# An expert stage's first block: empty products ahead of a gather's wait, a weight load ahead of it

## What is computed

```python
    le_g = jnp.take_along_axis(le, gsel[:, :, None], axis=1)[:, 0]
    ev, ei = lax.top_k(le_g, TOP_K)
    wts = jnp.take_along_axis(pg, gsel, axis=1) * jax.nn.softmax(ev, axis=-1)
    ...
    for e in range(N_EXPERTS):
        he = jax.nn.silu(h2 @ w_gate[e]) * (h2 @ w_up[e])
        out = out + combine[:, e:e + 1] * (he @ w_down[e])
```

## Time and profile before

| | us |
|---|---|
| median of 3 runs | 975.17 (972.69 to 975.19) |
| the profiled execution | 972.41 |
| its span in the profile | 970.6 |
| PE busy | 949.0 (98%) |
| VectorE busy | 700.3 (72%) |
| ScalarE busy | 493.1 (51%) |
| GpSimd busy | 190.1 (20%) |

### The profile page before, as it was taken

How to read it: one execution, slowest core, us unless ns; L and a number is a source line. 1 busy time by engine, 2 the same in 40 slices (tenths; PEclk the granted TensorE clock), 3 DMA queues, 4 the chain that set the end, 5 groups by cost and what they waited for, 6 DMA issues and landing times.

```text
span 970.6 us, 14838 instructions
## 1 busy us (share of the span) xinstructions
PE 949.0 (98%) x5402; PEld 818.1 (84%) x5402; DVE 700.3 (72%) x1063; ACT 493.1 (51%) x895; POOL 190.1 (20%) x153
## 2 busy tenths in 40 slices
PE   6999999999999999999999999999999999999996
PEld 5899999999999999999888886567777777777762
DVE  7467777789454544636666667779999999999986
ACT  7588777433322222322422314256666666666794
POOL 2000000000000000000030001325464646464414
PEclk9999999999999999999999999999999999999999
DMA  7214775524765554546833236899999999999994
GB/s 233 52 33 135 169 170 134 170 88 125 233 169 151 159 144 117 146 140 187 275 104 130 74 105 258 301 409 414 413 416 415 414 410 412 401 414 413 388 396 166
DMA packets 123477, 230.09 MB, mean 237 GB/s; under 512 B 71525, under 2 KB 84491, under 8 KB 114712
## 3 DMA queue, kind: packets, MB, share of 16 engines
q1 hardware_dynamic: 108078, 202.16, 60.2%
q0 software_dynamic: 15264, 26.92, 7.4%
q10 hardware_dynamic: 74, 0.20, 0.1%
HBM read 204.81 MB, written 53.11 MB: 266 GB/s over the span
## 4 chain that ended last, share of the span: by engine, by line
PE 92%; DMA 2%; DVE 2%; ACT 2%; issue 1%; POOL 1%; POOLq 0%; DVEq 0%; SPq 0%
PE psum L1184 34%; PE psum L2532 12%; PE psum L2181 9%; PE psum L2622 8%; PE psum L2536 5%; PE psum L2468 3%; PE psum L1207 2%; PE psum L2092 1%; PE psum L2516 1%; PE psum L2131 1%; PE psum L2589 1%; PE psum L1289 1%; PE psum L1276 1%; PE psum L1282 1%; PE psum L1293 1%
## 5 line engine op out<-in xcount | busy, mean ns | idle before, releaser
L1184 PE MATMUL psum<-hh,wh 128*128 128x350 f32 x672 | 222.9, 332 | 1.6 <-DVE hl L866 1.6
L1184 PE MATMUL psum<-hh,wl 128*128 128x350 f32 x672 | 217.6, 324 | 0.0
L1184 PE MATMUL psum<-hl,wh 128*128 128x350 f32 x672 | 216.9, 323 | 0.0
L1184 PEld LDWEIGHTS psum<-hh,wh 128*128 128x128 f32 x672 | 127.3, 189 | 3.0 <-issue 2.0
L1184 PEld LDWEIGHTS psum<-hl,wh 128*128 128x128 f32 x672 | 127.2, 189 | 0.9
L1184 PEld LDWEIGHTS psum<-hh,wl 128*128 128x128 f32 x672 | 127.0, 189 | 0.0
L2506 DVE TENSOR_TENSOR wgu_lo<-wgu,wgu_hi 128x1536 fp32r<-128x1536 f32 x60 | 105.4, 1758 | 18.1 <-ACT wgu_hi L2501 17.7
L2501 ACT ACTIVATE wgu_hi<-wgu 128x1536 fp32r<-128x1536 f32 x60 | 89.3, 1489 | 4.1 <-DMA new_ssm_sample<-s_in 4.1
L2532 PE MATMUL psum<-wgu_hi,xgt_hi 128*128 128x512 f32 x180 | 85.6, 475 | 0.0
L1742 POOL IOTA r_iw<- 128x8 f32 x1 | 0.1, 143 | 407.2 <-DMA mixer_rows<-th 407.2
L2532 PE MATMUL psum<-wgu_lo,xgt_hi 128*128 128x512 f32 x180 | 70.8, 393 | 0.0
(11 more groups left out here) (395 smaller groups left out, 1910.4 us busy)
## 6 DMA issues: line engine op xcount, KB each, us to landing
wgu<-w_gate SPq DMA_DIRECT2D x34, 1024.0 KB
wgu<-w_up SPq DMA_DIRECT2D x34, 1024.0 KB
wd<-w_down SPq DMA_DIRECT2D x34, 1024.0 KB, 15.2
wst<-w_in SPq DMA_DIRECT2D x28, 512.0 KB, 4.4
ck<-qkv_rows SPq DMA_DIRECT2D x9, 702.0 KB
qkv_rows<-acc SPq DMA_DIRECT2D x12, 520.0 KB, 5.9
xb<-x SPq DMA_DIRECT2D x8, 512.0 KB, 4.4
wo<-w_out SPq DMA_DIRECT2D x8, 512.0 KB, 6.7
```

The lines of the kernel that those rows point to most:

```text
L1184: ins = mm(ps[:, c, 0:ZC], w[:, kk, :], a[:, kk, c * ZC:(c + 1) * ZC], start=(kk == 0 and q == 0), stop=(kk == KD - 1 and q == 2))
```

## The change

On PE, block 0: all nine empty products run at the end of the router (before three there, four behind the turn), and `totals` runs ahead of the wait for the gather. The turn of block 0 signals after its first four transposes; ScalarE's first copy waits for that, its second for the whole turn. The signal uses the semaphore `ninth`, now named `passed`. `gate_up` gets an argument `halves`, with which it waits for one copy, then for the other at the middle; `mid` passes it for block 0. On SyncE, gate and up of the third expert are loaded before the wait for the gathers, behind the wait for the residual rows.

```diff
     def sync_more(sp):
+        sp.wait_ge(b.x1_out.sem, b.x1_out.at(16 * T))
+        load_gate_up(sp, b, io, expert_of(2), 2)
         for k in range(2):
             sp.wait_ge(b.gathered[k], 16)
         load_down(sp, b, io, expert_of(1), 1)
-        sp.wait_ge(b.x1_out.sem, b.x1_out.at(16 * T))
-        load_gate_up(sp, b, io, expert_of(2), 2)
         load_down(sp, b, io, expert_of(2), 2)
...
-        idle_products(pe, 3)
+        idle_products(pe, 9)
...
-    def turn(pe, q, k):
+    def turn(pe, q, k, half_turned=None):
...
+            if g == 0 and half_turned is not None:
+                ins.then_inc(half_turned, 1)
         ins.then_inc(q.turned.sem, 1)
...
-    def copy_turned(act, q, p, n):
-        act.wait_ge(q.turned.sem, q.turned.at(n + 1))
+    def copy_turned(act, q, p, n, half_turned=None):
+        if half_turned is None:
+            act.wait_ge(q.turned.sem, q.turned.at(n + 1))
+        else:
+            act.wait_ge(half_turned.sem, half_turned.at(4))
...
         for g in range(2):
+            if g == 1 and half_turned is not None:
+                act.wait_ge(q.turned.sem, q.turned.at(n + 1))
...
-    def gate_up(pe, q, p, n, k, part=range(KD)):
+    def gate_up(pe, q, p, n, k, part=range(KD), halves=False):
         if part[0] == 0:
-            pe.wait_ge(q.xt_ok.sem, q.xt_ok.at(2 * n + 2))
+            pe.wait_ge(q.xt_ok.sem, q.xt_ok.at(2 * n + (1 if halves else 2)))
         for kk in part:
+            if halves and kk == KD // 2:
+                pe.wait_ge(q.xt_ok.sem, q.xt_ok.at(2 * n + 2))
...
+                if isinstance(x.e, int) and x.e == 0:
+                    route.totals(pe)
                 pe.wait_ge(gathered[x.k], 16 * (x.r + 1))
-                turn(pe, x.q, x.k)
-                if isinstance(x.e, int) and x.e == 0:
-                    route.idle_products(pe, 4)
-                    route.totals(pe)
+                turn(pe, x.q, x.k, route.passed.sem if isinstance(x.e, int) and x.e == 0 else None)
...
             def mid(x):
...
-                    gate_up(pe, x.q, x.p, x.n, x.k)
+                    gate_up(pe, x.q, x.p, x.n, x.k, halves=isinstance(x.e, int) and x.e == 0)
```

More of the change, by code:

```diff
@@ L1643, in route_parts @@
                                                   s("rwf_ok"))
-    weighted, ninth, x1_1, sq_1 = (s.again("x1_weighted"), s.again("ninth_tile_parts"), s.again("x1_first_half"),
+    weighted, passed, x1_1, sq_1 = (s.again("x1_weighted"), s.again("tensor_passed"), s.again("x1_first_half"),
                                     s.again("x1_first_squares"))
@@ L1718, in sync @@
         residual_stored(sp, T - 2)
-        sp.wait_ge(ninth.sem, ninth.at(2))
+        sp.wait_ge(passed.sem, passed.at(2))
         load_gate_up(sp, b, io, expert_of(0), 0)
-        sp.wait_ge(ninth.sem, ninth.at(3))
+        sp.wait_ge(passed.sem, passed.at(3))
         load_down(sp, b, io, expert_of(0), 0)
@@ L2001, in vector @@
                 dve.wait_ge(x_in[0], 16 * (T // 2 + 1))
-                dve.wait_ge(ninth.sem, ninth.at(1))
+                dve.wait_ge(passed.sem, passed.at(1))
                 add_half(0).then_inc(x1_1.sem, 1)
@@ L2133, in last_products @@
                     if c == 1 and i in (3, 5):
-                        ins.then_inc(ninth.sem, 1)
-                ins.then_inc(ninth.sem if c == 0 else prod, 1)
+                        ins.then_inc(passed.sem, 1)
+                ins.then_inc(passed.sem if c == 0 else prod, 1)
         for t in range(T - 1):
@@ L2222, in route_parts @@
     f.vector_extra, f.vector_tables, f.tensor_extra = vector_extra, vector_tables, tensor_extra
-    f.idle_products, f.totals = idle_products, totals
+    f.totals, f.passed = totals, passed
     return f
@@ L2829, in front_ @@
                 else:
-                    copy_turned(act, x.q, x.p, x.n)
+                    copy_turned(act, x.q, x.p, x.n, route.passed if isinstance(x.e, int) and x.e == 0 else None)
             def half(x):
```

## The result

| | median us | runs | ratio to before (95% interval) |
|---|---|---|---|
| before | 975.22 | 20 | |
| after | 979.65 | 20 | 1.0049 (1.0026 to 1.0072) |

Single runs of most kernels here lie 10 us or more above the rest, and the ratios leave the farthest out, so a ratio can differ from that of the medians.

A forecast was written before the change was run, and what follows sets the result against it. The prediction took PE to bound the kernel (busy 98% of the span, 92% of the chain). Its terms, -1.87 (PE) + 2.5 (gather) + 1.3 (clock), summed to +1.9 us: 977.1 us, range 973.0 to 979.8.

The forecast's parts named there:

- the likeliest case: Whole kernel: 977.1 us, +1.9 on the median, between -0.5 and +2.9 us; chance 0.50.
- slower beyond 0.3%: Rival: first gather waits for all the new loads, landing 615.1; +3.9 us, or +5.6 with a second low stretch; chance 0.26.
- Steps (1) and (2), PE: First gather's landing to first gate and up product: empty products and totals move ahead, first copy starts earlier; -1.87 us.
- Step (3), room behind it: Later PE steps: VectorE's gated rows and third expert's low part come in time, so the 1.87 us gain passes on.
- the 0.1 us for block 0's gated rows: Second PE step of block 0: VectorE finishes `he` at 624.92, PE needs it at 625.02; it just fits.
- The room of 2.2 us at the third expert: Third expert's weights: VectorE's first low part ready by 638.5, PE takes it at 640.72.
- Step (4), the gather: Third expert's loads fill the DMA engines as the first gather is issued; it lands about 613.5, +2.5 us.
- the upper bound of +4.1: First gather: new loads end at 612.5, then the gather takes 2.6 us alone and lands at 615.1.
- the other half: Half of the 5.1 us full-queue cost, put on sharing the engines; little of it paid, since the load ends at 612.5.
- The rows of the running sum: Same sort of gather elsewhere in the trace: lands 2.6 us after issue at kernel's end, 7.7 to 8.6 in expert stage.
- Step (5), the clock: PE idle 3.1 us before the delayed landing, so a low clock stretch falls on the first products; +1.3 us.
- The load's lead: DMA engines gain about 2.5 us for the sample store and fourth expert; worth nothing, as PE doesn't wait for either.

The follow-up runs named there:

- e1_pe_part: The changed kernel with SyncE's order of before put back, so only the work on PE and ScalarE is moved; 974.11 us against 974.36, ratio 1.0007.
- e7: The kernel before, storing only 0.25 of the 2 MB of the sample state; 970.59 us against 973.75, ratio 0.9978.
- e3: As e1_pe_part, with the halves argument also passed in both product calls of `begin`; ratio to before 1.0013.
- e8: As e1_pe_part, storing only 0.25 of the 2 MB of the sample state; 971.15 us against 973.75 for before, ratio 0.9971.
- e2: The kernel before with only SyncE's order changed: third expert's gate and up ahead of the wait for the gathers; 976.95 us against 974.36, ratio 1.0038.
- e4: The changed kernel with only the third expert's gate (1 MB) ahead of the wait for the gathers; 977.33 us against 974.36, ratio 1.0004.
- e11: The kernel before with one more 2 MB DMA copy on SyncE near the end of the expert stage; 982.2 us against 974.01, ratio 1.0077.

## Why the prediction was wrong

The range of 973.0 to 979.8 held 979.65, but the likeliest case, a loss of 1.9 us that can't be told from no change, was wrong: the case "slower beyond 0.3%" with its 0.26 came true, and with the mechanism written there in the main: the gather was held up by the new loads beyond the point given. Only it didn't wait for the whole of them, its packets began while they still ran. Point by point:

- **Steps (1) and (2), PE**: forecast -1.87 us from landing to first product. e1_pe_part has 2.01 us there for the 1.83 forecast, so -1.69, right to 0.2 us; `begin` without `halves` cost 0.5 us as said. But 1.24 of it was the removal of a low stretch which not every execution has, as e7 shows; the forecast compared a start at the lower clock with one at the full clock and priced it as if each execution had it.
- **Step (3), room behind it**: the 0.1 us for block 0's gated rows was about right (e3 waits 0.35 with 0.5 more asked). "So a gain of 1.87 passes on" was the wrong sentence. I looked for the next late step up to block 2 and not at the end, where the DMA engines set the time: the earlier trace rows give DMA 2% of the chain, and I read that as PE alone. The room of 2.2 us at the third expert was right for a gain of 1.87 alone. In e1 the second low stretch was missing too, so PE came 3.5 us earlier and waited 1.25 for VectorE's low part. That part starts at R 31.8 in both kernels, since ScalarE waits there for the 2 MB sample store, which landed at R 30.3 in both:

```profile
640.77 0.47 PE L2541 MATMUL psum<-wgu_hi,xgt_hi 128*128 128x512 f32 x1 [1.25 <-DVE wgu_lo L2513]
```

- **Step (4), the gather**: the term that was mis-sized, and the main failure. +2.5 forecast, +4.9 measured (8.87 for 3.96), and above the upper bound of +4.1. The wait for data ahead came out as forecast, 2.6 measured up to the first packet for 2.55 (half of 5.1), by luck, since the halves were a guess. "Little of" the other half was wrong, with +2.3 measured. The bound let the load end at 612.5 and gave the gather 2.6 us alone from there; in fact it had the rest of the load and the later gathers beside it, and took 4.4 us from its first packet. The rows of the running sum, 7.7 to 8.6 us under a full queue, were the better estimate as they stood: 8.87, 8.38 and 7.85 in three kernels.
- **Step (5), the clock**: +1.3 forecast. In the profile of after the way from the turn of block 0 to that of block 1 took 8.85 us, against 5.48 in e8 at the full clock: +3.4. The stretch was three times 3.4 us, where the forecast had one and left a second open. Whether the longer idle time (5.5 us and not 3.1) or the missing products behind the turn made it so isn't shown: e2, idle for 6.5 us with these products in place, had two. By the ratios the share is about 2 us.
- **The sum** by what was measured from the router's table: -1.69 + 4.91 + 3.37 = +6.6, as the trace has it at block 1's turn, and +6.0 at the end. The medians give +4.4 to 4.8, since the clock's part differs from one execution to the next (that this is all of the difference isn't shown).
- The load's lead was put at nothing. No run takes it alone; where PE sets the end, as in after with its 65.8 us, none of it shows. The doubt about the direction was in the rivals: the point from which slower decides (a landing of 614.1, or 613.5 with two low stretches) was reached by a wide margin: 618.12, less 2.18 of upstream shift, is 615.9.

## What to carry to other kernels

A transfer for which an engine waits is worth more than the bandwidth beside it: 2 MB of weights issued 1.2 us ahead of a gather delayed it by 4.9 us, and 1 MB by 1.35, so let bulk loads wait for it, or make them small. Size such a delay by the same kind of transfer under load elsewhere in the trace, not by the mean rate of the engines: even the end of the load doesn't free them if more gathers have queued up meanwhile. And before a gain is summed through to the end, look what sets the end: here PE made up 92% of the chain of waits, and in the profile 2 us won on PE were lost again in waits for the last loads, behind DMA engines that had been full since 616.

## What the runs showed that I had not expected

- With 2 MB of weights ahead of it the gather's queue had no packet for 4.4 to 4.5 us after the issue, whether the weights came in packets of 8 KB or of 4 KB; with 1 MB for 2.7 us, with nothing for 1.9.
- 2 MB of extra copy near the end cost 7.5 us, 1.5 times the 5 us that it would be at the 424 GB/s of a full window (an estimate); the final loads came 5 us later and the stretch behind them grew too.
- The clock fell after 2.05 us of idle time in the profile of before and after 1.91 in e4, and stayed up after 1.86 us in e7 and 1.82 in e11, which have the order of before. One profile of before therefore doesn't tell whether a low stretch belongs to the kernel.
